# Two-block model on one core: attention worked through in quads of two query heads and both key heads, with plain transposes

## The reference, cut to what matters

```python
s = jnp.einsum('bgrcd,bgnd->bgrcn', qc, kc) * ATTN_SCALE
p_cmp = masked_softmax(s, cmp_end[None, :] <= tpos[:, None])
o_cmp = jnp.einsum('bgrcn,bgnd->bgrcd', p_cmp, vc.astype(jnp.float32))
...
s = jnp.einsum('bgrcd,bgcnd->bgrcn', qc, ksel) * ATTN_SCALE
o_slc = jnp.einsum('bgrcn,bgcnd->bgrcd', masked_softmax(s, m_slc), vsel.astype(jnp.float32))
...
s = jnp.einsum('bgrcd,bgnd->bgrcn', qc, kw) * ATTN_SCALE
o_win = jnp.einsum('bgrcn,bgnd->bgrcd', masked_softmax(s, m_win), vw.astype(jnp.float32))
out = gc[..., 0:1] * o_cmp + gc[..., 1:2] * o_slc + gc[..., 2:3] * o_win
```

## Time and profile before

| | |
|---|---|
| Median of 3 runs | 2669.78 us (2666.0 to 2677.55) |
| The profiled execution | 2671.9 us, span 2669.8 us |
| Mean granted TensorE clock | 0.951 |
| Attention, first scores to last value product | 191.4 to 608.7 us |
| Experts at full DMA rate | from about 1670 us to the end |

### The profile page before, as it was taken

The page is one execution under the profiler, slowest core; times in us unless marked ns, Lnnn a source line. Parts: engine busy times, 40 slices in busy tenths (PEclk is TensorE's granted clock), DMA queues, the critical chain, the costliest instruction groups (busy, mean ns, idle before and its releaser), DMA issues.

```text
span 2669.8 us, 21453 instructions
## 1 busy us (share of the span) xinstructions
PE 2399.3 (90%) x8764; PEld 1155.5 (43%) x8764; DVE 639.5 (24%) x1374; ACT 323.2 (12%) x670; POOL 167.7 (6%) x155
## 2 busy tenths in 40 slices
PE   7998989899999999999999999998878788888786
PEld 4654444444454554445764445533333233333232
DVE  2243342434144223003252113311111111111113
ACT  2012222221011110002101002100000000000001
POOL 0000000000104330000000000000000000000001
PEclk9998999899999999999878999999999999899998
DMA  6210101012222322121722332999999999999995
GB/s 250 98 45 6 57 1 63 3 42 99 95 111 96 114 98 88 63 95 68 122 91 95 118 126 108 386 427 425 427 425 426 426 427 426 424 425 425 422 412 225
DMA packets 69859, 552.50 MB, mean 207 GB/s; under 512 B 20984, under 2 KB 25208, under 8 KB 38336
## 3 DMA queue, kind: packets, MB, share of 16 engines
q1 hardware_dynamic: 43104, 514.44, 47.4%
q10 hardware_dynamic: 16576, 24.28, 3.1%
q0 software_dynamic: 10080, 12.38, 1.3%
HBM read 543.91 MB, written 35.68 MB: 217 GB/s over the span
## 4 chain that ended last, share of the span: by engine, by line
PE 62%; DMA 21%; DVE 5%; ACT 2%; SPq 1%; issue 1%; ACTq 0%; DVEq 0%; POOL 0%; POOLq 0%
PE ps L382 17%; DMA sb<-in_eu 11%; PE ps L990 9%; PE ps L697 7%; PE ps L458 6%; DMA sb<-in_eg 6%; PE ps L1019 4%; DMA sb<-in_ed 3%; PE ps L629 2%; PE ps L840 2%; PE ps L401 2%; PE ps L577 2%; PE ps L780 2%; PE ps L547 2%; PE ps L569 1%
## 5 line engine op out<-in xcount | busy, mean ns | idle before, releaser
L382 PE MATMUL ps<-sb 128*128 128x512 f32 (+2 forms) x1536 | 619.2, 563 | 9.1 <-DVE sb L1935 4.4
L990 PE MATMUL ps<-sb 128*64 128x512 f32 x2048 | 482.1, 626 | 100.0 <-DMA sb<-in_eu 68.8
L382 PEld LDWEIGHTS ps<-sb 128*128 128x128 f32 x1536 | 282.0, 192 | 329.8 <-issue 318.4
L990 PEld LDWEIGHTS ps<-sb 128*64 128x64 f32 x2048 | 176.2, 144 | 385.1 <-issue 385.1
L1019 PE MATMUL ps<-sb 128*64 128x512 f32 x992 | 237.6, 635 | 36.3 <-DMA sb<-in_ed 23.9
L458 PE MATMUL ps<-sb 128*128 128x512 f32 x512 | 248.3, 615 | 0.0
L697 PE MATMUL ps<-sb 128*128 128x512 f32 x448 | 192.5, 592 | 0.7 <-issue 0.7
L1019 PEld LDWEIGHTS ps<-sb 128*64 128x64 f32 x992 | 78.4, 145 | 174.0 <-issue 153.5
L1420 DVE TENSOR_TENSOR sb<-sb 128x32 f32<-128x32 f32 (+10 forms) x324 | 119.3, 383 | 133.2 <-PE ps L663 83.2
L697 PEld LDWEIGHTS ps<-sb 128*128 128x128 f32 x448 | 85.0, 190 | 107.7 <-issue 107.7
L458 PEld LDWEIGHTS ps<-sb 128*128 128x128 f32 x512 | 91.9, 197 | 78.3 <-issue 77.8
(11 more groups left out here) (281 smaller groups left out, 1782.3 us busy)
## 6 DMA issues: line engine op xcount, KB each, us to landing
sb<-in_eg SPq DMA_DIRECT2D x64, 2048.0 KB, 33.1
sb<-in_eu SPq DMA_DIRECT2D x62, 2048.0 KB, 33.8
sb<-in_ed SPq DMA_DIRECT2D x62, 2048.0 KB, 33.9
sb<-in_m SPq DMA_DIRECT2D x16, 2048.0 KB, 7.3
sb<-in_mg SPq DMA_DIRECT2D x8, 1536.0 KB, 6.2
sb<-in_winF SPq DMA_DIRECT2D x5, 2048.0 KB, 7.7
sb<-in_mgg SPq DMA_DIRECT2D x4, 2048.0 KB, 7.9
sb<-in_wo SPq DMA_DIRECT2D x4, 2048.0 KB, 7.8
```

Of the source, the lines that this page charges most:

```text
L382: ins = pe.matmul(out, lhsT, rhs, start=k == 0, stop=k == len(pieces) - 1)
L990: ins = pe.matmul(o[64 * e:64 * e + 64, :], x[:, k, 64 * e:64 * e + 64], weight(2 * mat + e)[:, 512 * k:512 * k + 512], start=k == 0, stop ...
```

## The change

Work is listed as 16 quads (i, jp, ty): two query columns 2 jp and 2 jp + 1, both heads, one ty. Each quad has two parts u, one per query column, with both heads' scores, so that the two score matmuls of a part use different partitions and banks. i is now the outer loop. The mask matmul is replaced by an addition on VectorE in PSUM ahead of the maximum. The diagonal matrices are gone: VectorE multiplies the probabilities by gate / sum in place, and TensorE uses its plain transpose, four per 128 keys (two columns by two heads) into one bank. The copies cover 512 columns each and alternate between ScalarE and VectorE; there are 40. The value products are one matmul of 256 columns per head, the two heads alternating between the two halves of bank 7's partitions. The compressed probabilities and values of head 1 are kept in partitions 32 to 62, so VectorE copies the compressed values in two pieces. `PR` has four buffers in place of two. Attention takes 124 steps in place of 128.

The diff, cut to its core:

```diff
-        PCT = view(zone, z1, 8, 512)
+        PCT = view(zone, z1, 4, 512)
...
-        PR = [zal(2, 512) for _ in range(2)]
+        PR = [view(zone, z1 + 2048 + 1024 * n, 2, 512) for n in range(2)] + [zal(2, 512) for _ in range(2)]
...
-        UNITS = [(j, i, h) for j in range(4) for i in range(4) for h in range(2)]
+        QUADS = [(i, jp, ty) for i in range(4) for jp in range(2) for ty in range(2)]
+        PTN = [(q, kb) for q, (i, jp, ty) in enumerate(QUADS) for kb in range(i + 1)]
+        PTC = {t: c for c, t in enumerate(PTN)}
```

TensorE:

```diff
-                def scores(n):
-                    j, i, h = UNITS[n]
-                    nk = 128 * (i + 1)
-                    hs = slice(64 * h, 64 * h + 64)
-                    for ty in range(2):
-                        o = open_tile(pe, ("s", n, ty), 2 + 2 * (n % 2) + ty)
-                        pe.matmul(o[:, 0:nk], qT[hs, j, 128 * i:128 * i + 128], kT[hs, ty, 0:nk], start=True, stop=False)
-                        pe.matmul(o[:, nk - 128:nk], ident, ck("neg"), start=False, stop=True).then_inc(T.f("s", n, ty), 1)
-                    yield 1
+                def scores(u):
+                    i, jp, ty = QUADS[u // 2]
+                    j, nk = 2 * jp + u % 2, 128 * (i + 1)
+                    o = [open_tile(pe, ("s", u, h), 2 + 2 * (u % 2) + h) for h in range(2)]
+                    for h in range(2):
+                        hs = slice(64 * h, 64 * h + 64)
+                        pe.matmul(o[h][:, 0:nk], qT[hs, j, 128 * i:128 * i + 128], kT[hs, ty, 0:nk],
+                                  start=True, stop=True).then_inc(T.f("s", u, h), 1)
+                    yield 2
 
                 pe.wait_ge(*T.free("k", 0))
                 pe.wait_ge(*T.free("k", 1))
...
                 for n in range(8):
                     pe.wait_ge(*T.free("ct", n // 2, n % 2))
                 yield from scores(0)
-                for n, (j, i, h) in enumerate(UNITS):
-                    hd = 4 * h + j
-                    hs = slice(64 * h, 64 * h + 64)
-                    if n + 1 < len(UNITS):
-                        yield from scores(n + 1)
-                    for ty in range(2):
-                        pt = open_tile(pe, ("pt", n, ty), 6)
-                        pe.wait_ge(*T.free("s", n, ty))
-                        pe.wait_ge(S("dg"), 2 * n + ty + 1)
-                        for kb in range(i + 1):
-                            ins = pe.matmul(pt[:, 128 * kb:128 * kb + 128], PR[n % 2][:, ty, 128 * kb:128 * kb + 128],
-                                            DG[n % 2][:, ty, :], start=True, stop=True)
-                        ins.then_inc(T.f("pt", n, ty), 1)
+                yield from scores(1)
+                for q, (i, jp, ty) in enumerate(QUADS):
+                    if q + 1 < len(QUADS):
+                        yield from scores(2 * q + 2)
+                        yield from scores(2 * q + 3)
+                    if q % 4 == 0:
+                        open_tile(pe, ("o", i), 7)
+                    ob = T.ap("o", i)
+                    for kb in range(i + 1):
+                        c = PTC[(q, kb)]
+                        pt = open_tile(pe, ("pt", c), 6)
+                        for jj in range(2):
+                            if kb == 0:
+                                pe.wait_ge(S("prob"), 2 * q + jj + 1)
+                            for h in range(2):
+                                ins = pe.transpose(pt[:, 128 * (2 * h + jj):128 * (2 * h + jj) + 128],
+                                                   PR[(2 * q + jj) % 4][:, h, 128 * kb:128 * kb + 128], ident)
+                        ins.then_inc(T.f("pt", c), 1)
                         yield 1
-                        if n % 8 == 0 and ty == 0:
-                            ob = open_tile(pe, ("o", j), 7)
-                        pe.wait_ge(*T.free("pt", n, ty))
-                        for kb in range(i + 1):
-                            ins = pe.matmul(ob[hs, 128 * i:128 * i + 128], Vn[:, kb, 128 * ty + 64 * h:128 * ty + 64 * h + 64],
-                                            PTR[ty][:, 128 * kb:128 * kb + 128], start=ty == 0 and kb == 0, stop=False)
+                        pe.wait_ge(*T.free("pt", c))
+                        for h in range(2):
+                            ins = pe.matmul(ob[64 * h:64 * h + 64, 256 * jp:256 * jp + 256],
+                                            Vn[:, kb, 128 * ty + 64 * h:128 * ty + 64 * h + 64],
+                                            PTR[c % 2][:, 256 * h:256 * h + 256], start=ty == 0 and kb == 0, stop=False)
                         ins.then_inc(S("pv"), 1)
-                    ins = pe.matmul(ob[hs, 128 * i:128 * i + 128], vc[0:31, 64 * h:64 * h + 64], PCT[0:31, hd, 128 * i:128 * i + 128],
-                                    start=False, stop=True)
-                    if n % 8 == 7:
-                        ins.then_inc(T.f("o", j), 1)
-                    yield 1
+                    if ty == 1:
+                        for h in range(2):
+                            ins = pe.matmul(ob[64 * h:64 * h + 64, 256 * jp:256 * jp + 256], vc[32 * h:32 * h + 31, :],
+                                            PCT[32 * h:32 * h + 31, 2 * jp:2 * jp + 2, 128 * i:128 * i + 128], start=False, stop=True)
+                        if jp == 1:
+                            ins.then_inc(T.f("o", i), 1)
+                    yield 2 if i == 3 else 1
```

ScalarE:

```diff
-                def scores(n):
-                    j, i, h = UNITS[n]
+                def scores(u):
+                    i, jp, ty = QUADS[u // 2]
                     nk = 128 * (i + 1)
-                    act.wait_ge(S("smax"), n + 1)
-                    if n > 1:
-                        act.wait_ge(*T.full("pt", n - 2, 1))
-                    for ty in range(2):
-                        act.activation(PR[n % 2][:, ty, 0:nk], T.ap("s", n, ty)[:, 0:nk], ACT.Exp, bias=ST[n % 2][:, ty:ty + 1],
-                                       scale=0.125, accum_out=ST[n % 2][:, 2 + ty:3 + ty]).then_inc(T.s("s", n, ty), 1)
                     yield 1
+                    act.wait_ge(S("smax"), u + 1)
+                    if u > 3:
+                        act.wait_ge(*T.full("pt", PTC[(u // 2 - 2, QUADS[u // 2 - 2][0])]))
+                    for h in range(2):
+                        act.activation(PR[u % 4][:, h, 0:nk], T.ap("s", u, h)[:, 0:nk], ACT.Exp, bias=ST[u % 2][:, h:h + 1],
+                                       scale=0.125, accum_out=ST[u % 2][:, 2 + h:3 + h]).then_inc(T.s("s", u, h), 1)
+                    yield 1
 
                 yield from scores(0)
-                for n, (j, i, h) in enumerate(UNITS):
-                    nk = 128 * (i + 1)
-                    if n + 1 < len(UNITS):
-                        yield from scores(n + 1)
-                    for ty in range(2):
-                        if ty == 0:
-                            if n:
-                                act.wait_ge(S("pv"), 2 * n - 1)
-                            copy(("pt", n, 0), PTR[0][:, 0:nk], T.ap("pt", n, 0)[:, 0:nk])
+                yield from scores(1)
+                for q, (i, jp, ty) in enumerate(QUADS):
+                    if q + 1 < len(QUADS):
+                        yield from scores(2 * q + 2)
+                        yield from scores(2 * q + 3)
+                    for kb in range(i + 1):
+                        c = PTC[(q, kb)]
+                        if c % 2 == 0:
+                            if c > 1:
+                                act.wait_ge(S("pv"), c - 1)
+                            copy(("pt", c), PTR[0])
                         yield 1
-                    yield 1
+                    yield 2 if i == 3 else 1
```

VectorE:

```diff
-                def scores(n):
-                    j, i, h = UNITS[n]
-                    nk = 128 * (i + 1)
-                    hd = 4 * h + j
-                    st = ST[n % 2]
+                def scores(u):
+                    i, jp, ty = QUADS[u // 2]
+                    j, nk = 2 * jp + u % 2, 128 * (i + 1)
+                    st = ST[u % 2]
                     mx, rs = st[:, 0:2], st[:, 2:4]
-                    dve.wait_ge(*T.full("s", n, 0))
-                    dve.wait_ge(*T.full("s", n, 1))
-                    if n > 1:
-                        dve.wait_ge(S("dg"), 2 * n - 2)
-                    b = 2 + 2 * (n % 2)
+                    gcol = gate[:, i, :].rearrange("p (h j c) -> p h j c", h=2, j=4)[:, :, j, 1 + ty]
+                    b = 2 + 2 * (u % 2)
                     both = PS[:, 512 * b:512 * b + 1024].rearrange("p (a b) -> p a b", a=2)
+                    dve.wait_ge(*T.full("s", u, 0))
+                    dve.wait_ge(*T.full("s", u, 1))
+                    after(tt(both[:, :, nk - 128:nk], both[:, :, nk - 128:nk], bc(ck("neg"), 1, 2), ALU.add))
                     after(own(dve.tensor_reduce(mx, both[:, :, 0:nk], op=ALU.max, axis=AX.X)))
                     dve.tensor_scalar(mx, mx, -0.125, None, ALU.mult).then_inc(S("smax"), 1)
```

(60 more changed lines are left out.)

2 lines of the change are left out of this document (1 added, 1 removed).

## The result

The changed kernel takes 2603.7 us (median of 4, 2599.9 to 2604.7) against 2670.4 us before; the ratio is 0.9745, with a 95% interval of 0.9722 to 0.9769. That is 66.6 us less, where 54 were forecast. The profiled execution took 2604.7 us.

The account below looks back on a forecast made before the run. TensorE was taken to bound the dense attention stretches and the in-order VectorE-ScalarE chain those at the `gr` tiles. -64 outside, +10 for waits and clock and 0 at the tiles gave -54 us, 2616 us, range 2585 to 2648.

Parts of the forecast that it names:

- TensorE's work, -94: Attention stage: TensorE's scores, transposes, value products and compressed values go from 178 to 84 us, 94 us less.
- the list of signs: What traces should show, among others: score pair 0.4 + nk/512 x 0.43 us, value pair 0.43, stretch about 54 us shorter.
- VectorE, +23: Attention stage: VectorE gains mask additions and products, loses diagonal scalings and copies; 154 to 177 us, costing no throughput.
- What is given back: TensorE's 30 us saving at the `gr` tiles turns into waiting; about 10 us more go to waits and lower clock.
- I take these 145 us as unchanged (bounds: 15 us shorter, 15 longer): Stretches 230:280, 335:380 and 500:550, holding six `gr` tiles: TensorE's saving becomes waiting on VectorE's chain, so length stays.
- Outside, one for one: The 88 attention steps away from the `gr` tiles: TensorE's saved work counts fully, 94 x 88/128 = 64 us.
- At 512 keys it is 25 us against 12: covered: Outside the `gr` tiles: a quad's attention and recurrent steps take 25 us, enough to cover its 12 us chain.
- The gr stretches shrink too: Rival: TensorE runs ahead of VectorE at `gr` tiles, up to the whole 94 comes through; middle -80, 2590 us; chance 0.17.
- The clock rival: Rival: less work between waits lowers TensorE's clock; half the dense stretches' 208 us at 1.2 GHz gives 2720; chance 0.04.
- signs of a wrong forecast: Pairs running in series, idle outside the `gr` stretches above 20 us, or the clock there below 0.95.
- No change, or slower: Rival: freed time is all given back at waits of the first small quads and `gr` tiles, within 0.5%; chance 0.05.

Follow-up runs that it names:

- long_first: Changed kernel with the query blocks in falling order, quads of 512 keys first and 128 last: 2606.6 us, ratio 0.9758.
- no_reciprocal: Changed kernel without VectorE's reciprocal in the recurrence, results wrong: time (4127 us) not comparable, stretch 337.2 us against 357.5.
- values_serial: Changed kernel with both heads' selected and window value products written to the same half of the partitions, so they can't overlap: 2619.4 us, ratio 0.9812.
- scores_serial: Changed kernel with both score matmuls of a part taken from head 0's partitions, so they can't run side by side: 2613.4 us, ratio 0.9788.
- full_matmul_transposes: Changed kernel with each plain transpose made an f32 matmul with the identity, two passes for one: 2613.4 us, ratio 0.9789.
- first_block_early: Changed kernel with each quad's first transposed block and its copy put between the two parts of the next quad's softmax: 2587.5 us, ratio 0.9698.
- copies_on_scalar: Changed kernel with all 40 copies of transposed probabilities on ScalarE: 2583.2 us, ratio 0.9674.

## Why the prediction was right, and where its sizes were off

The forecast was -54 us, the result -66.6, inside the range and of the sign; 12.6 us of the size were missed.

- *TensorE's work, -94.* Measured -95 (360 to 265). By line, from the matmuls' starts at full clock: scores with masks 69.7 to 23.0 us (forecast 73 to 30), transposes 40.3 to 19.8 (35 to 17), value products 43.7 to 22.6 (58 to 32), compressed values 11.3 to 4.4 (11.5 to 4.6); in sum 165 to 70, where the forecast had 178 to 84. The columns held (0.43 us for a value pair), and so did the overlap of the row halves, which no row had shown. The gaps did not: 0.2 us a score pair for 0.4, and 0.15 a value group for 0.38, while a transpose with its share of gaps took 0.124 us for 0.109. The value groups were priced too high on both sides, so most of that drops out of the difference, and the rest evens out, which is partly luck. One slip: the list of signs gives a pair's length as nk/512 x 0.43; the sum used 0.85, and 0.85 is right.
- *VectorE, +23.* Its own terms add up to 22. Measured +22.4 (159.0 to 181.4), mask 0.429 us each, products 26.4 us in all.
- *What is given back.* This is the term that was mis-sized. The forecast gave back 40 of the 94, the chip 27 of the 95: 21 idle and 5.5 in the clock. The split was off by more. I cut the changed kernel's trace at the same dense matmuls at which the forecast's stretches begin and end. "I take these 145 us as unchanged (bounds: 15 us shorter, 15 longer)" became 117, 28 less: against 50, 45 and 50 us in the earlier trace rows the three now read

```profile
223.10:248.50 25.40, 21.05 (x69) 9.08 (x68) 18.72 (x37) 10.72 (x23) 0.00 (x0) 0.87 0.15 53
301.80:350.30 48.50, 29.55 (x81) 11.58 (x79) 29.85 (x48) 14.08 (x28) 0.00 (x0) 0.75 0.00 1
459.00:502.30 43.30, 30.12 (x90) 11.97 (x89) 28.65 (x39) 12.83 (x20) 0.00 (x0) 0.80 0.07 25
```

  Nearly all of it lies at the first pair of tiles, where quads of 128 keys make VectorE's chain short. long_first shows that this is the cause: between those tiles the interval fell from 27.0 to 17.1 in the changed kernel, and with long quads there it is 24.6.
- *Outside, one for one.* Outside those three stretches the forecast was -64 and +10 for waits, -54; measured are -41 (272.3 to 231.5). It failed most in the interval 361.7:509.0, which lost 9.8 us though TensorE's work in it fell by 34: idle there went from 7 to 22 us, and the clock's loss from 2 to 11. "At 512 keys it is 25 us against 12: covered" counted the chain's length and not who stands in front of whom; the copies behind the next quad's exponentials wait for all of it. In 264.7:337.6, 13 us came through of 18. Only the first interval (46.3 to 32.7) and the last (78.0 to 55.1) paid in full. In the last one the scores end at 504.7, and behind them almost no softmax is left to stand in front of a copy; that this is the reason is not shown. What the sum had right is that VectorE's chain, and not TensorE, prices most `gr` bursts; no_reciprocal shows it. The two errors, 28 us too little at the tiles and 13 too much outside, partly cancel. That the total lies so near is in this part luck.
- *The gr stretches shrink too.* This rival (-80 in the middle) was right at the first pair of tiles and wrong at the other two. The measured -66.6 lies about halfway between the forecast and it.
- *The clock rival.* The loss grew by 5.5 us, where that rival needed 54 and more. But in the forecast's own stretches the clock outside the `gr` tiles fell from 1.00 to 0.90 and 0.92 in two of four (the other two stayed at 0.79 and 1.00), and idle there rose from 6 to 25 us, both of which I had named as signs of a wrong forecast. They were the signs of the wrong split, with the sum made up elsewhere. The Trainium skill (TensorE: Matmul & The Clock Gate, Part 4, PE-mode transpose) has it that transposes don't count as activity. The two measured losses, 31.5 us with transposes and 30 without, show no cost of that here.
- *No change, or slower.* Not seen anywhere in the traces.

A microsecond of TensorE's work was worth 0.7 of stretch in the change and 0.6 to 0.75 in the three experiments that put 17 to 20 us back. With the copies moved it would perhaps be worth more; that wasn't tried.

## What to carry to other kernels

When in-order engines pass work to each other, look for a short operation whose input is long ready and that sits behind another stage's wait: moving it forward, or to the queue that isn't the late one, gave 51 us of the stretch here, where 95 us less of matmul work gave 69. Matmuls of 64 rows or 64 columns should come in pairs on opposite halves and without full-size ones between them: here a pair took 1.05 us in place of 1.91, and its switches cost 0.15 to 0.2. And after a bound engine is relieved, price the second one by its chain, with sizes as they meet in time, not by its mean busy time.

## What I had not expected of the hardware

The stretch ahead of attention, with the same TensorE instructions up to there, took 191 to 194 us in most profiled executions and 201 in four. Of those 7 us, 5.5 are in one place. In TensorE's timeline of the changed kernel it reads

```profile
109.85 7.33 PE L381 MATMUL ps<-sb 128*128 128x62 f32 x64 [1.38 <-issue]
```

and in values_serial

```profile
110.40 12.80 PE L381 MATMUL ps<-sb 128*128 128x62 f32 x64 [1.39 <-issue]
```

The same 64 passes of 62 columns behind the same idle of 1.4 us: 7.33 us in one, 12.80 in the other, where the clock of 100:125 us is granted at 0.73 and not at 1.00. It shows in scores_serial, values_serial, full_matmul_transposes and long_first, and not in the others. Each kernel has one trace, so whether it belongs to the execution or to the kernel is open; in the first three of these kernels the profiled execution is also the slowest, by 4 to 8 us, which speaks for the execution. It is 0.3% of the time, so a single execution can't rank two kernels as close as that.

Shorter waits also give time back through the clock, at no fixed rate: first_block_early saved 6 us of idle and 13 of clock, copies_on_scalar 15 and 9. And two f32 matmuls on opposite row halves overlap fully even as an isolated pair of 128 to 512 columns (0.42 and 1.05 us with 0.2 of gaps).
